# Chunked recurrence of an RWKV-7 layer: one PSUM bank set apart for the outputs' product, three for the other four products of a chunk

## What is computed

```
def step(S, inp):
    w_t, k_t, v_t, kk_t, a_t = inp[:5]
    s_kk = jnp.einsum('nbhvk,nbhk->nbhv', S, kk_t)
    S = S * w_t[..., None, :] - s_kk[..., :, None] * (kk_t * a_t)[..., None, :] + v_t[..., :, None] * k_t[..., None, :]
    y_t = jnp.einsum('nbhvk,nbhk->nbhv', S, inp[5]) if emit else None
    return S, y_t
```

## Time and profile before

| | |
|---|---|
| median of 3 runs | 5104.01 us (5098.47 to 5106.06) |
| profiled execution | 5095.65 us |
| span of its trace | 5093.9 us |
| PE busy | 4834.0 us (95% of the span) |
| DVE busy, ACT busy | 1474.9 us (29%), 1053.9 us (21%) |
| the scan | about 2960 to 3524 us from the span's start |
| PE busy, DVE busy in the scan | 480.42 us, 377.44 us of 564 |
| granted TensorE clock, whole and scan | 0.971, 0.95 of full speed |

### The profile page before, as it was taken

One profiled execution on the slowest core, in us unless ns is written; L12 is line 12 of the kernel. 1 busy time (PEld: TensorE's weight loads), 2 busy tenths in 40 slices (PEclk: granted clock), 3 DMA queues, 4 the chain that ended last, 5 costly groups with the idle time before them and its releaser, 6 DMA issues.

```text
span 5093.9 us, 63120 instructions
## 1 busy us (share of the span) xinstructions
PE 4834.0 (95%) x27502; PEld 2657.5 (52%) x27502; DVE 1474.9 (29%) x2777; ACT 1053.9 (21%) x2046; POOL 321.5 (6%) x302
## 2 busy tenths in 40 slices
PE   8999999999999999999998988888999999899999
PEld 4444444444444445665454567776544555544444
DVE  3621110462211000000424257774202444410100
ACT  1231000123100012110313133432112333311210
POOL 1100000110000000000014000000000110000000
PEclk9999999999999999999999999998999999989999
DMA  3151212124122201111234322122111000011211
GB/s 120 72 192 67 74 67 83 59 83 179 69 74 70 79 33 66 50 50 46 78 128 140 114 86 73 59 73 93 60 55 43 28 28 19 39 42 63 86 74 58
DMA packets 91841, 378.36 MB, mean 74 GB/s; under 512 B 7985, under 2 KB 33713, under 8 KB 62129
## 3 DMA queue, kind: packets, MB, share of 16 engines
q1 hardware_dynamic: 80608, 332.92, 18.4%
q0 software_dynamic: 9808, 37.75, 2.2%
q10 hardware_dynamic: 1152, 3.67, 0.2%
HBM read 334.46 MB, written 39.85 MB: 73 GB/s over the span
## 4 chain that ended last, share of the span: by engine, by line
PE 90%; DVE 5%; ACT 2%; issue 2%; DMA 0%; POOL 0%; POOLq 0%; SPq 0%; DVEq 0%; ACTq 0%
PE ps L521 43%; PE ps L333 23%; PE ps L542 7%; PE ps L3385 2%; PE ps L1781 2%; PE ps L339 1%; PE ps L3312 1%; PE ps L990 1%; PE ps L946 1%; PE ps L3396 1%; PE ps L2477 1%; PE ps L3315 1%; PE ps L3311 1%; PE ps L3313 1%; PE ps L979 0%
## 5 line engine op out<-in xcount | busy, mean ns | idle before, releaser
L521 PE MATMUL ps<-A,W 128*128 128x512 f32 (+1 forms) x5408 | 2175.2, 562 | 24.4 <-DVE A L493 8.8
L521 PEld LDWEIGHTS ps<-A,W 128*128 128x128 f32 x5408 | 1028.9, 192 | 1119.2 <-issue 1076.5
L333 PE MATMUL ps<-A,W 64*64 64x64 f32 (+3 forms) x3264 | 668.1, 383 | 44.2 <-DVE R L2936 17.4
L333 PEld LDWEIGHTS ps<-A,W 128*128 128x128 f32 (+2 forms) x3264 | 354.7, 164 | 338.1 <-issue 306.2
L333 PE MATMUL ps<-A 64*64 64x64 f32 (+3 forms) x8416 | 454.1, 241 | 63.6 <-ACT A L3538 23.2
L333 PEld LDWEIGHTS ps<-A 64*64 64x64 f32 (+2 forms) x8416 | 416.3, 151 | 165.9 <-issue 96.6
L542 PE MATMUL ps<-W,A 128*128 128x512 f32 (+1 forms) x896 | 366.0, 570 | 1.8 <-ACT A L1567 1.8
L542 PEld LDWEIGHTS ps<-W,A 128*128 128x128 f32 x896 | 172.0, 193 | 191.2 <-issue 183.9
L435 ACT ACTIVATE A<-R 128x512 f32<-128x512 f32 (+1 forms) x96 | 52.6, 574 | 782.4 <-DVE R L1577 354.6
L1697 DVE SCALAR_TENSOR_TENSOR A<-ps,V,A 128x512 f32<-128x512 f32 (+1 forms) x48 | 31.0, 660 | 486.9 <-PE ps L333 486.4
L1577 DVE SCALAR_TENSOR_TENSOR R<-ps,MOD,R 128x512 f32<-128x512 f32 (+1 forms) x48 | 31.7, 661 | 439.5 <-PE ps L521 438.2
(11 more groups left out here) (358 smaller groups left out, 4162.0 us busy)
## 6 DMA issues: line engine op xcount, KB each, us to landing
W<-in_ada SPq DMA_DIRECT2D x48, 1024.0 KB, 5.6
W<-in_w_up SPq DMA_DIRECT2D x44, 1024.0 KB, 4.8
W<-in_w_down SPq DMA_DIRECT2D x32, 704.0 KB, 4.1
W<-in_w_in SPq DMA_DIRECT2D x18, 1024.0 KB, 4.9
W<-in_sgu_v SPq DMA_DIRECT2D x16, 1024.0 KB, 4.9
W<-in_sgu_u SPq DMA_DIRECT2D x16, 1024.0 KB, 4.8
W<-in_sgu_z SPq DMA_DIRECT2D x16, 1024.0 KB, 4.9
W<-in_sgu_o SPq DMA_DIRECT2D x16, 1024.0 KB, 4.8
```

Source lines behind the costliest of these rows:

```text
L333: r = e.matmul(out, a, b, start=start and i == 0, stop=stop and i == len(pairs) - 1, skip_group_check=loose)
L521: t = e.matmul(ps, w[:, k, c:c + mc], x(k, seg), start=k == 0, stop=k == kt - 1)
```

## The change

Y gets bank 7 for itself. X, both U and P go round banks 4, 5 and 6.

```
-        ps = take(pl, ("X", u), "4567")
+        ps = take(pl, ("X", u), "456")
...
-        y = take(pl, ("Y", u), "4567")
+        y = take(pl, ("Y", u), "7")
         e.wait_ge(*free(pl, ("Y", u)))
...
-        ps = [take(pl, x, "4567") for x in names]
+        ps = [take(pl, x, "456") for x in names]
...
-        ps = take(pl, ("P", u), "4567")
+        ps = take(pl, ("P", u), "456")
```

## The result

The changed kernel takes 5049.93 us (median of 4 runs, 5047.67 to 5060.9) against 5101.24 us before (4 runs): a ratio of 0.9904, 95% interval 0.989 to 0.9918. The profiled execution takes 5050.79 us, 44.9 less than that of before, with a span of 5049.0 us.

The account below looks back on a forecast made before the run. PE was taken to bound the kernel, standing still for Y's removal. Gains of 15.5 + 2.6 + 7.6 + 4 = 29.7 us, taken from the median 5104.01, gave 5074.3 us; range 5058 to 5092.

Parts of the forecast that it names:

- which wait goes: In the scan, X stops waiting for DVE to read the earlier Y; the wait moves to Y's first matmul.
- what is late next: First chunks, steps 1 to 9: blocks then wait for the bank ACT empties, starting 1.57 us sooner than before.
- The 22 waits: PE's waits in the scan for DVE's lines 2936 and 2938, 29.5 us; to fall to one or two.
- 15.5 + 2.6 + 7.6: Gains in us from shorter waits: first chunks of steps 1 to 9, second chunks of steps 0 to 9, last two steps.
- The 2.6 for second chunks: Steps 0 to 9: nine waits of 0.29 us before second chunks go, 2.6 us, or 0 if DVE's work is late.
- the clock term: Last two steps: shorter waits save 4 us of the 12.3 us lost to a lower PE clock; bounds 0 and 12.3.
- Regular waits leave the granted clock at 1.00: In the scan's regular steps, PE's waits were taken to cost no clock, which stays at 2.4 GHz.
- I take a third, 4 us: Last two steps: the share of the 12.3 us of lost clock that shorter waits were taken to save.
- the clock stays up: Rival: whole 12.3 us of clock back in the last two steps, 1 to 3 elsewhere; gain 37 to 41 us; chance 0.13.
- Supply gaps: Rival: PE meets 3.26 us instruction gaps behind X in about half of nine steps; gain about 16 us; chance 0.12.
- the slower one: Rival: a 3.26 us instruction gap at each of 22 places, 39 us slower, 5143; chance 0.03.
- The wait did not merely move: Rival denied here: blocks or DVE's work late in X's place, only last two steps pay, 5096 to 5104; chance 0.10.

Follow-up runs that it names:

- the filled kernel: Changed kernel with PE again waiting for the earlier chunk's Y before every X, but multiplying constants into X's bank meanwhile: 5076.83 us, ratio 0.9937.
- the 0.82 above: Granted clock at the end of the scan in the changed kernel with the wait put back before second chunks of steps 0 to 9 only: 5070.44 us, one run.
- the regular waits alone put back: Changed kernel with PE's wait for the earlier Y put back before first chunks of steps 1 to 9 only: 5085.44 us, ratio 0.9956.
- reordered: Changed kernel with PE's order altered so that its remaining short waits have work of the same strand in front of them: 5051.4 us, ratio 0.99.

## Why the prediction was right and wrong

**Right: which wait goes, and what is late next.** The 22 waits went as worked out; the blocks start at ACT's end plus 0.14; DVE's idle time fell to 1.50 (1.6 was forecast); only the last step keeps a wait at Y, 0.41 us where 1.35 was expected (a gap of 0.73 us inside X took up part of it). Regular steps fell by 2 us, as forecast. In one direction they went from 43.81 to 42.06 us at a clock of 1.00, which is 1.75, the share of the first chunk alone. In the other they went from 45.4 us at 0.96 to 41.6; laid beside the 43.8 of the filled kernel at 1.00, that is 2.2. The waits by themselves were put at 15.5 + 2.6 + 7.6 = 25.7 us; the kernel with filled waits against the changed one gives 23.2. The 2.6 for second chunks came near 2.9 to 3.4 by luck: the prediction took 0.29 us in every step or nothing, and it was 0.5 in one half of the steps and 0.1 in the other.

**Wrong: the clock term.** The step that failed is "Regular waits leave the granted clock at 1.00", and with it "I take a third, 4 us". The first was read from one window of 16 us in one step. Over all nine steps the kernel before shows 0.98, and that 0.02 hides 6.9 us of longer records. Two of its steps, one after the other, show what one window cannot:

```profile
3096.57:3140.38 43.81, 38.60 (x992) 34.15 (x993) 33.47 (x56) 17.71 (x36) 2.17 (x2) 1.00 0.27 75
3140.38:3185.78 45.40, 40.06 (x992) 35.49 (x993) 32.96 (x56) 17.60 (x36) 2.18 (x2) 0.96 0.26 72
```

They hold a first-chunk wait for Y of 1.86 and 1.85 us; the second ran its 992 records at 0.96 and took 1.6 us longer, 1.5 of it as PE's busy time. The end gave back 10.7 us, nearly all of the 12.3 that stood as its upper bound, though waits of 1.89 and 3.03 us stay in it; in another execution it need not have, as the 0.82 above shows. So 17.6 us, by PE's busy time, stood against 4. The rival "the clock stays up" had the right mechanism and place for the end, and 1 to 3 us for what is 6.9 in the regular steps; its 37 to 41 us came nearest of all. The rule of the Trainium skill ("TensorE: Matmul & The Clock Gate", "A second HAM failure mode: psum-queue depth-cycling") was set aside too soon: with the regular waits alone put back, nine steps have a clock of 0.96, and with them filled 1.00. The trace agrees with the rule there, though not for every short stop: waits of 0.8 to 1.4 us for masks and exponentials stay in the changed kernel's nine steps, and each of these shows 1.00.

25.7 of waits and 17.6 of clock would be 43.3; the two profiled executions differ by 44.9. The medians differ by 51.3, with an interval, by the ratio's, of 42 to 56, which holds the 44.9. The last 6 us are no term of the change that a trace shows: the profiled execution of before was 5.6 us under its median. The prediction noted that and took its gain off the median all the same. With a gain of 44.9 this gives 5059, just inside the range, so how far below it the time fell is in part chance; that the clock term was too small by 13.6 us is not.

**The other rivals.** Supply gaps did not grow (10.2 us against 11.2), so neither the case of part of the gain lost to them nor the slower one came. The gap of 3.26 us went the other way: in the step that holds it, "issue" is 3.8 us before, and 6.5 and 4.8 with regular waits put back (all of them, first chunks alone). With the waits gone or filled, five traces, it is 1.0 to 1.6. Why was not tried. The wait did not merely move. That Y has one bank alone cost 0.41 us in 24 chunks.

**What stays open.** Why a given stretch loses its clock and the next, with the same waits, does not. For the nine steps the runs show that the waits bring the falls. For the end they leave it likely: it fell in all three traces with its waits (0.86, 0.79, 0.83), but also, to 0.82, in one of five without them; the others show 0.98, 0.98, 1.00 and, reordered, 0.94. With the waits filled it stayed at 1.00.

## What to carry to other kernels

A bank ring whose takes per round are one more than its banks ties each round's first product to the round before's second, here the one that was read last; give the product that stays open longest a bank of its own, and check that the wait then stands behind work that covers it. When PE's waits are what a change removes, price the clock too: take PE's busy time and granted clock over the whole stage, not over one good window, because each small fall hides as longer records and not as idle time. And to learn what a wait costs beside its length, fill it with products that nobody reads and leave it in place.

## What had not been expected of the hardware

With one wait of 1.6 to 1.9 us in nearly every step of some 44 us, the granted clock of a step stayed at 1.00 or fell below it: of 27 steps in the three kernels with these waits (the one before, all waits back, regular waits back), 16 show 0.92 to 0.97 and 11 show 1.00, in the kernel before in turn. All 45 steps with these waits gone (36, four traces) or filled by products (9) show 1.00. And the fall is not the same from one execution to the next: one end of the scan of the same PE instructions took 89.2, 90.7 and 103.1 us, at clocks of 1.00, 0.98 and 0.82, the last with one wait of 0.29 us put back ahead of it.
